# Squares of five norms summed in four bands of 32 output partitions, added one page later

## What is computed

```python
def rmsnorm_2(x, g):
    x32 = x.astype(jnp.float32)
    y = x32 * lax.rsqrt(jnp.mean(x32 * x32, axis=-1, keepdims=True) + EPS)
    return (y * g.astype(jnp.float32)).astype(x.dtype)

def modulate_2(x, g, shift, scale):
    return rmsnorm_2(x, g) * (1 + scale) + shift

def macaron_ffn(xs, g, shift, scale, gate, w_gate, w_up, w_down):
    return xs + 0.5 * gate * swiglu(modulate_2(xs, g, shift, scale), w_gate, w_up, w_down)
```

## Time and profile before

| | us |
|---|---|
| median of 3 runs | 2015.49 |
| lowest and highest | 2014.15, 2018.49 |
| the profiled execution | 2017.46 |
| its span, first to last instruction | 2015.7 |
| TensorE busy | 1955.8 (97%) |
| GpSimd busy | 1304.1 (65%) |
| VectorE busy | 1001.8 (50%) |
| ScalarE busy | 805.8 (40%) |
| mean granted TensorE clock | 0.990 |

### The profile page before, as it was taken

One profiled execution on the slowest core, in us unless ns is written; L12 is line 12 of the kernel. 1 busy time (PEld: TensorE's weight loads), 2 busy tenths in 40 slices (PEclk: granted clock), 3 DMA queues, 4 the chain that ended last, 5 costly groups with the idle time before them and its releaser, 6 DMA issues.

```text
span 2015.7 us, 34549 instructions
## 1 busy us (share of the span) xinstructions
PE 1955.8 (97%) x13934; PEld 1775.3 (88%) x13934; DVE 1001.8 (50%) x2158; ACT 805.8 (40%) x872; POOL 1304.1 (65%) x311
## 2 busy tenths in 40 slices
PE   6999899999999999999999999899999999999998
PEld 4879788877767899999999678799999999999998
DVE  6766455765755554445336435453344334654112
ACT  3443343344445543344333323443344334334332
POOL 5727167766566677777774312387768776867784
PEclk9999899999999999999999899999999999999999
DMA  8537167778987556666664212266666665655442
GB/s 351 220 129 292 61 270 283 303 307 338 364 345 289 222 226 235 245 238 227 240 252 187 105 43 84 105 230 235 239 214 230 239 240 209 251 209 200 178 186 84
DMA packets 63957, 448.74 MB, mean 223 GB/s; under 512 B 7680, under 2 KB 8800, under 8 KB 9824
## 3 DMA queue, kind: packets, MB, share of 16 engines
q1 hardware_dynamic: 61888, 441.65, 58.1%
q10 hardware_dynamic: 1952, 5.44, 0.7%
HBM read 446.01 MB, written 1.05 MB: 222 GB/s over the span
## 4 chain that ended last, share of the span: by engine, by line
PE 53%; issue 23%; POOL 18%; DMA 4%; DVE 1%; ACT 1%; POOLq 0%; SPq 0%; ACTq 0%; DVEq 0%
POOL W L665 15%; PE bank L742 11%; PE bank L744 11%; PE bank L743 11%; DMA raw<-in_pages 3%; PE bank L1194 3%; PE bank L1262 3%; PE bank L1195 3%; PE bank L1202 2%; POOL YC L718 2%; PE bank L768 1%; PE bank L777 1%; PE bank L1137 1%; PE bank L788 1%; PE bank L807 1%
## 5 line engine op out<-in xcount | busy, mean ns | idle before, releaser
L665 POOL TENSOR_TENSOR W<-raw,W 128x2048 fp32r<-128x2048 f32 x220 | 1013.8, 4614 | 516.5 <-ACT W L1561 516.4
L742 PE MATMUL bank<-YH,W 128*128 128x256 f32 x1936 | 551.2, 285 | 1.1 <-POOL W L665 0.8
L744 PE MATMUL bank<-YH,W 128*128 128x256 f32 x1936 | 547.6, 283 | 0.0
L743 PE MATMUL bank<-YL,W 128*128 128x256 f32 x1936 | 547.6, 283 | 0.0
L1561 ACT ACTIVATE W<-raw 128x2048 fp32r<-128x2048 f32 x220 | 420.1, 1909 | 302.0 <-PE bank L744 275.6
L742 PEld LDWEIGHTS bank<-YH,W 128*128 128x128 f32 x1936 | 371.0, 192 | 3.9 <-POOL W L665 1.2
L743 PEld LDWEIGHTS bank<-YL,W 128*128 128x128 f32 x1936 | 371.2, 192 | 0.4 <-issue 0.2
L744 PEld LDWEIGHTS bank<-YH,W 128*128 128x128 f32 x1936 | 371.1, 192 | 0.0
L1916 DVE SCALAR_TENSOR_TENSOR bank<-mraw,CA,bank 128x256 f32<-128x256 f32 x696 | 328.9, 488 | 19.8
L2013 DVE TENSOR_TENSOR bank<-bank,SIL 128x256 f32<-128x256 f32 x110 | 47.6, 432 | 540.2 <-ACT SIL L1580 540.2
L742 PE MATMUL bank<-HH,W 128*128 128x256 f32 x880 | 249.7, 284 | 0.5 <-DVE HL L2015 0.4
(11 more groups left out here) (383 smaller groups left out, 3088.9 us busy)
## 6 DMA issues: line engine op xcount, KB each, us to landing
raw<-in_pages SPq DMA_DIRECT2D x284, 1024.0 KB, 4.8
mraw<-in_mpages SPq DMA_DIRECT2D x98, 1024.0 KB, 6.9
R<-in_pages SPq DMA_DIRECT2D x20, 1024.0 KB, 7.1
XR<-in_pages SPq DMA_DIRECT2D x12, 1024.0 KB, 6.1
R<-in_mpages SPq DMA_DIRECT2D x4, 1024.0 KB, 16.3
HT<-in_acts ACTq DMA_DIRECT2D x1, 1024.0 KB, 14.2
CT<-in_mpages SPq DMA_DIRECT2D x1, 1024.0 KB, 19.3
raw<-in_mpages SPq DMA_DIRECT2D x1, 1024.0 KB, 25.1
```

The source lines that it names most:

```text
L665: nc.gpsimd.tensor_tensor(WL[:, p % SLOTS, :], raw[:, p % SLOTS, :], WH[:, p % SLOTS, :].bitcast(f32), ALU.subtract).then_inc(s_lo, 1)
L742: mm(out, w[0], x[0], start=start, stop=False, skip_group_check=True)
L743: mm(out, w[0], x[1], start=False, stop=False, skip_group_check=True)
L744: return mm(out, w[1], x[0], start=False, stop=stop, skip_group_check=True)
```

## The change

Norms 2 to 6 get their sum in another way. The eight products use 32 columns of ONES and write to four bands of 32 partitions of the bank, tile k to band k % 4, so that each band holds a quarter of the sum. ScalarE copies the bank to XR[:, 0, :], and one product with the whole of ONES adds the bands up. Each quarter then counts 32 times, which the root's scale divides out. That last product stands a page later: for norm 2 a job later, for 3, 4 and 5 after page 0 of the next unit, for 6 at the end of the projection kac0, whose last quarter of products follows the groups. The root of 3, 4 and 5 stands after silu 0 of that unit.

The tiles of norms 3, 4 and 5, and the squares of norm 4, move one unit later on ScalarE and VectorE, and the groups of norm 2 one job earlier. Norm 2's bank is 7 (MISC) in place of 5; in place of the last-but-one scatter it waits for the last modulation sum of the experts. The first four units of ff00 are unrolled, where two were.

```diff
--- before.py
+++ after.py
@@ -329,6 +329,7 @@
                                                   sem("group_aux"), sem("group_aux_copied"))
         s_silu = sem("silu_done")
         s_sq = sem("norm_squares")
+        s_grp, s_grpd = sem("norm_groups_summed"), sem("norm_groups_copied")
         s_rt, s_ri, s_xr, s_yf, s_y = (sem("norm_root"), sem("norm_coef"), sem("norm_scaled"), sem("norm_result"),
                                          sem("norm_split"))
         s_xs = sem("norm_plain")
@@ -416,7 +417,7 @@
         tile("ss1", 1, (MISC,), "act")
         tile("rt", 1, (0,), "dve")
         tile("rtt", 1, (0,), "dve")
-        tile("ss2", 1, (5,), "act")
+        tile("ss2", 1, (MISC,), "act")
         tile("acc_moe", 4, (2, 3, 0, 1), "dve")
         tile("ss3", 1, (MODB,), "act")
         tile("ss4", 1, (MODB,), "act")
@@ -525,6 +526,9 @@
 
         SPLITS = [sum(1 for x in NORMS[:n] if x[1] in OPERANDS) for n in range(len(NORMS) + 1)]
         N_SMALL, N_MID = 10, 4
+        GROUPED = (2, 3, 4, 5, 6)
+        NG4, GW = 4, P // 4
+        TOTAL_IN = {("ctx_ff", 1): 3, ("ctx_ff", 3): 4, ("ff00", 2): 5}
         MID_NORM = {"ctx_ff": ((1, "ss3"), (3, "ss4")), "ff00": ((2, "ss5"),), "ff01": (), "ff10": (), "ff11": ()}
 
 
@@ -535,7 +539,8 @@
                 ("ctx_ff", FF_UNITS, "yc", "acc_ctx", ((1, (ONE, BOTH)), (1, (BOTH, ONE)), (1, (ONE, BOTH)), (1, (BOTH, ONE)),
                                                             (2, (BOTH, BOTH)), (1, (ONE, BOTH)), (1, (ONE, ONE)),
                                                             (1, (BOTH, ONE)), (1, (BOTH, BOTH)), (1, (ONE, BOTH)))),
-                ("ff00", FF_UNITS, "y", "acc_00", ((1, (ONE, ONE)), (1, (ONE, ONE)), (FF_UNITS - 2, (ONE, ONE)))),
+                ("ff00", FF_UNITS, "y", "acc_00", ((1, (ONE, ONE)), (1, (ONE, ONE)), (1, (ONE, ONE)), (1, (ONE, ONE)),
+                                                          (FF_UNITS - 4, (ONE, ONE)))),
                 ("ff01", FF_UNITS, "y", "acc_01", ((2, (ONE, ONE)), (FF_UNITS - 2, (ONE, ONE)))),
                 ("ff10", FF_UNITS, "y", "acc_10", ((2, (ONE, ONE)), (FF_UNITS - 2, (ONE, ONE)))),
                 ("ff11", FF_UNITS, "y", "acc_11", ((2, (ONE, ONE)), (2, (ONE, ONE)), (FF_UNITS - 4, ())))):
@@ -782,6 +787,22 @@
                 for c in range(NCH):
                     norm_chunk(n, c)
 
+            def norm_groups(n):
+
+                ps = opened(pe, f"ss{n}")
+                pe.wait_ge(s_sq, NCH * (n + 1))
+                for k in range(KD):
+                    rows = slice(GW * (k % NG4), GW * (k % NG4 + 1))
+                    last = mm(ps[rows, 0:S], ONES[:, 0:GW], XR[:, k, :], start=(k < NG4), stop=(k >= KD - NG4),
+                              skip_group_check=True)
+                last.then_inc(s_grp, 1)
+
+            def norm_total(n):
+
+                pe.wait_ge(s_grpd, GROUPED.index(n) + 1)
+                mm(bank(f"ss{n}")[:, 0:S], ONES[:], XR[:, 0, :], start=True, stop=True, skip_group_check=True)\
+                    .then_inc(s_tile, 1)
+
             def stay_awake(n):
 
                 for _ in range(8):
@@ -808,7 +829,7 @@
                                   skip_group_check=True)
                 return last
 
-            def linear(p, ps, x, ready=None, k_tiles=KD, wcol=FU, off=0, inc=True):
+            def linear(p, ps, x, ready=None, k_tiles=KD, wcol=FU, off=0, inc=True, behind=None):
 
                 w = shaped([a[:, 0:k_tiles * wcol] for a in arrived(p)], "p (k n) -> p k n", k=k_tiles)
                 for b in range(2):
@@ -816,6 +837,8 @@
                     for k in range(k_tiles):
                         if ready is not None and b == 0:
                             ready(k)
+                        if behind is not None and b == 1 and k == k_tiles // 2:
+                            behind()
                         last = mm3(ps[:, b * S:(b + 1) * S], [a[:, k, c:c + P] for a in w], [a[:, k, :] for a in x],
                                    k == 0, k == k_tiles - 1)
                 if inc:
@@ -850,6 +873,8 @@
                                 last = mm3(PS[GU[j]][:, g * S:(g + 1) * S], [a[:, k, g, :] for a in w],
                                            [a[:, k, :] for a in x], k == 0, k == KD - 1)
                         last.then_inc(s_page, 1)
+                        if j == 0 and (name, u) in TOTAL_IN:
+                            norm_total(TOTAL_IN[name, u])
                     if vectors:
                         for at_unit, ss in MID_NORM[name]:
                             if u >= at_unit:
@@ -1300,23 +1325,26 @@
                         gather(j + 1, e - 5)
                     elif e == 7:
                         aux(j + 1)
+                if t == NJOB - 4:
+                    pe.wait_ge(s_macc, MOD_AT["ctx_ff"])
+                    norm_groups(2)
                 if t == NJOB - 3:
-                    pe.wait_ge(s_scd, 4 * (GSLOTS - 2))
-                    norm(2)
+                    norm_total(2)
             turn_hid(NJOB - 1)
             down(NJOB - 1)
 
 
             def mid_norm(name, u, n):
                 pe.wait_ge(s_modev, MOD_AT[name] + u - 1)
-                norm(n)
+                norm_groups(n)
 
             ff_pass("ctx_ff", 2, (lambda: mid_norm("ctx_ff", 1, 3), lambda: None, lambda: mid_norm("ctx_ff", 3, 4)))
             ff_pass("ff00", 4, (lambda: None, lambda: mid_norm("ff00", 2, 5)))
             mod_product(MOD_AT["mixer"] - 1)
 
-            linear(PA["proj_a"], opened(pe, "kac0"), YC, inc=False, ready=lambda k: y_ready(5, k)).then_inc(s_tile, 1)
-            norm(6)
+            linear(PA["proj_a"], opened(pe, "kac0"), YC, inc=False, ready=lambda k: y_ready(5, k),
+                   behind=lambda: norm_groups(6)).then_inc(s_tile, 1)
+            norm_total(6)
             linear(PA["proj_a"] + 1, opened(pe, "kac1"), YC, inc=False).then_inc(s_tile, 1)
             for q in range(2):
                 linear(PA["proj_a"] + q, opened(pe, "kax", q), Y, ready=(lambda k: y_ready(6, k)) if q == 0 else None)
@@ -1540,7 +1568,12 @@
 
             def norm_root(n):
                 ps = filled(act, f"ss{n}")
-                free(f(RT[:, 0:S], ps[:, 0:S], ACT.Sqrt, bias=EPSC[:, 0:1], scale=1.0 / D), f"ss{n}")
+                copies = GW if n in GROUPED else 1
+                free(f(RT[:, 0:S], ps[:, 0:S], ACT.Sqrt, bias=EPSC[:, 0:1], scale=1.0 / (D * copies)), f"ss{n}")
+
+            def norm_groups_copy(n):
+                act.wait_ge(s_grp, GROUPED.index(n) + 1)
+                f(XR[:, 0, :], bank(f"ss{n}")[:, 0:S], ACT.Copy).then_inc(s_grpd, 1)
 
             def norm_scaled(n, ks=range(KD)):
                 src, dst, _, _, sc, sh, vi = NORMS[n]
@@ -1580,6 +1613,8 @@
                         f(SIL[:, j, :], PS[GU[j]][:, 0:S], ACT.Silu).then_inc(s_silu, 1)
                         if p + j + SLOTS < RPAGES:
                             split(p + j + SLOTS, i)
+                        if j == 0 and (name, u) in TOTAL_IN:
+                            norm_root(TOTAL_IN[name, u])
                     if p + 2 + SLOTS < RPAGES and not (u == n - 1 and name in TAIL):
                         split(p + 2 + SLOTS, i)
 
@@ -1673,7 +1708,7 @@
             after(PA["wout"] + 3)
 
             def state_norm():
-                norm_result(3)
+                norm_scaled(3)
                 norm_squares(4)
 
             def expert_split(u, part):
@@ -1760,6 +1795,8 @@
                     act.wait_ge(sem("in_ctx"), 16)
                     act.wait_ge(s_gdown, 32)
                     norm_squares(2)
+                if t == NJOB - 4:
+                    norm_groups_copy(2)
                 if t == NJOB - 3:
                     norm_root(2)
                 if t == NJOB - 2:
@@ -1772,9 +1809,9 @@
             after(PA["ctx_ff"] - 1)
             out_copy(GSLOTS - 1)
             norm_squares(3, "acc_moe")
-            ff_pass("ctx_ff", (state_norm, lambda: None, lambda: norm_result(4)))
+            ff_pass("ctx_ff", (lambda: norm_groups_copy(3), state_norm, lambda: norm_groups_copy(4), lambda: norm_scaled(4)))
             norm_squares(5, "acc_ctx")
-            ff_pass("ff00", (lambda: None, lambda: norm_result(5)))
+            ff_pass("ff00", (lambda: None, lambda: norm_groups_copy(5), lambda: norm_scaled(5)))
             norm_squares(6, "acc_00")
 
             for dst, src in ((BT0, small["bt"][:, 0:BTN]), (BT1, small["bt"][:, BTN:]), (CSB, small["csb"]),
@@ -1792,8 +1829,10 @@
             def key_half(nm, i, q, c):
                 free(f(KA[:, 2 * q:2 * q + 2, c * S:(c + 1) * S], two(filled(act, nm, i)), ACT.Copy), nm, i)
 
+            norm_groups_copy(6)
+            norm_root(6)
             key_half("kac0", 0, 0, 1)
-            norm_result(6)
+            norm_scaled(6)
             key_half("kac1", 0, 1, 1)
             for q in range(2):
                 key_half("kax", q, q, 0)
@@ -2419,9 +2458,9 @@
             residual("acc_moe", (HT, modcol(ADA + 40)))
 
 
```

(4 more changed lines are left out.)

## The result

The changed kernel takes 2017.68 us (median of 12 executions, 2015.97 to 2026.42), the kernel before, in the same session, 2013.77 (12 executions, 2009.86 to 2022.35). The ratio is 1.0026, with a 95% interval from 1.0014 to 1.0038: slower by some 5 us (3.9 by the two medians) where 5.4 less were forecast.

A forecast was written before the change was run, and what follows sets the result against it. TensorE was taken as the bound from 664 to 1110 us. Norms 2 to 6 gave -1.5, -0.3, +0.1, -1.9 and -1.8, together -5.4 us, from the median 2015.49 to 2010.1; range 2005.5 to 2018.0.

The forecast's parts named there:

- Part 1: Norm sums on TensorE: 3.45 us replaced by 1.1 for groups and 0.45 for the total, saving 1.9 a norm.
- bands apart: Rival at the eight narrow products: bands don't run side by side, loads and products queue; 2021.9 us, chance 0.16.
- pairs only: Rival at the eight narrow products: only pairs overlap, 1.95 us a norm; 2014.4 us, no change, chance 0.12.
- the first rival: Same as bands apart: weight loads stand between the narrow products, which keep 3.45 us; 2021.9 us, chance 0.16.
- The copy and the root: ScalarE's 0.4 us copy is hidden in feed-forward passes; the root between two silus needs 5.4 us of 5.76 and fits.
- Part 2: Norms 3 and 4, tiles one unit later: hidden tile at +20.3, TensorE at +18.3, a 2.0 us wait at each.
- NA_: VectorE's gain column, between modulation sum and reciprocal: taken at its median 1.1 us, minimum 0.16, maximum 3.8.
- Part 3: Norms 2, 5 and 6: norm 5 hides by 0.8 us and gains 1.9; norm 6 gains 1.8, norm 2 1.5.
- +17.1: Norm 5 in ff00: us after silu 1 when the hidden tile is ready, against TensorE's arrival at +17.9.
- Norm 6: Keeps its place; squares end just when the groups want them, so 0.1 us is taken off: gain 1.8.
- Norm 2: Groups a job earlier add no wait; 0.4 us lost to the hidden copy before the down product, gain 1.5.
- The clock: Rival at TensorE's 2.0 us waits: a stall lowers the granted clock, one fall giving 2013.1 us; chance 0.15.

The follow-up runs named there:

- bands: Changed kernel with norm 3's narrow products all in one band and norm 4's in two; only its trace is used: 3.57, 1.85 and 1.00 us at norms 3, 4, 5.
- quarters: Changed kernel with each GpSimd subtraction cut into four pieces from ctx_ff on; ratio to the kernel before 0.9991.
- before_held: Kernel before, with only GpSimd held back until VectorE has made the tiles of norms 3, 4 and 5; ratio to the kernel before 1.0028.
- awake: Changed kernel with 17, 17 and 10 small products of ones on TensorE ahead of the waiting units' modulation products; ratio to the kernel before 1.0001.
- held: Changed kernel, but before's tile places, groups after page 1, total inside the down product, root before the last split, GpSimd waiting for the eight tiles; 2005.30 us, ratio 0.9954.
- early_q: Like held, but GpSimd does not wait for the tiles; its subtraction is cut into four pieces from ctx_ff on instead; ratio to the kernel before 1.0015.
- held_again: The kernel held run once more, unchanged; 2006.12 us, ratio to the kernel before 0.9963.

## Why the prediction was wrong

- **The sums** (Part 1): right. 1.19 for the groups (1.1 taken) and 0.43 for the total (0.45 taken), in place of 3.45, save 1.8 a norm, 1.9 forecast. The rivals "bands apart" and "pairs only" fall with bands. The Trainium skill ("TensorE: Matmul & The Clock Gate", Part 3) gives 2.38 times for three column tiles; four gave 3.57 / 1.00 = 3.6 times here. The same part says that a weight load overlaps products only on another row group. Read so, the first rival and its 3.45 us would have come true; the trace, with 1.00, doesn't bear it out for loads into different column bands.
- **The copy and the root**: right. The copy of the groups takes 0.36 us, nobody waits for it, and the root ends between the two silus with 0.9 us to spare (silu 1 at 698.03 waits for TensorE).
- **The tiles of norms 3 and 4** (Part 2): here the sum failed. The mechanism was right, the size was not: 4.04 and 4.03 in place of 2.0. The term is NA_, 3.75 us in place of 1.1, 2.65 too little. I took the median of its durations, 1.1, as if it were a matter of chance, with 3.8 as the far bound. It is no chance: it is what is left of GpSimd's instruction when VectorE gets there, and the phase of the two is fixed by the order of the work. The changed kernel shows 3.75 both times; quarters shows the same place with 0.43 and a wait of 2.22. I had the spread of a factor of twenty on a row and did not ask what VectorE waited for. The other 0.6 went the other way, by the same cause: the tiles' times were taken from rows of before, where the first tile already stood 0.55 us behind GpSimd (1.82 us for three tiles at 727.88, 1.28 for the same three in before_held). In the changed kernel this part was free. All else in the count was met: the sum's end at +9.0, TensorE at +18.3.
- **Norm 5** (Part 3): wrong, 2.42 us of wait where 0.8 to spare were forecast. NA_ took the 1.09 I had counted, but the first tile lost 3.7 us behind GpSimd, of which 0.55 was in the rows already: 3.7 - 0.55 - 0.8 = 2.4. I had written that it could cost up to 2 with a long NA_, and left it out of the sum. The +17.1 there is also not what its terms add up to, which is 16.75; it came out right because the one-vector sum ends at +5.9 (926.47 to 932.36) and not at +5.5. That is luck.
- **Norm 6**: -1.3 in place of -1.8. The Y products came 2 us earlier and met VectorE's low parts, 0.79 us a tile: three waits where before had one. **Norm 2**: some -1.9 by the distance above, -1.5 forecast. In the traces with four bands the distance is 25.4 to 25.9, in the three with the sum of before 28.5 to 28.9. That nothing hides the groups is not shown.
- **The clock**: put down as a rival in place of the forecast, for one fall. It was put at nothing in the sum, and it came on top, at both long waits: 3.7 us in the first trace, 8.3 in the second (there at norm 5 too), and some 5 by awake. After waits of 2.0 to 2.4 us it fell in some traces too (in quarters at norms 4 and 5, not at 3), so even the forecast's own waits of 2.0 would have cost it at times.
- **Sum.** With the measured terms: norms 3 and 4 +7.4, norm 5 +0.6, norm 6 -1.2 make +6.8; measured between the marks, +6.6. With norm 2 it is +4.7, beside +3.9 by the medians and +5.2 by the ratio. What turned -5.4 into this is the waits behind GpSimd, +4.1 at norms 3 and 4 and +2.4 at norm 5, and the clock, +3.7. The measured 2017.68 lies just inside the range, whose upper end was kept for pairs with a long NA_, or two falls of the clock. The clock did fall twice, but on waits twice as long as forecast, and beside a third at norm 5: the range held it by its width, not by its reasons.

What VectorE waits for is told by all traces alike: instructions with two SBUF inputs (the gain column, the tiles) stand until GpSimd's instruction is over; the modulation sum, with its running sum in PSUM, goes at 0.455 us a step beside GpSimd (700.68 + 5.46 for twelve, across 700.30 + 4.62), and so does the reciprocal. The Trainium skill says so ("SBUF — State Buffer", section "Who interferes with whom"): VectorE and GpSimd share a port pair as an exclusive lock for a whole instruction, and a VectorE instruction with two SBUF inputs contends for it with a GpSimd instruction that reads SBUF, as the subtraction does. The traces agree, with 3.75, 4.21 and 5.01 us.

## What to carry to other kernels

Where a small VectorE instruction has durations between 0.16 and 3.8 us, find whose instruction it ends with before taking a mean; then count it by the phase that the changed order gives. Time taken off the bound engine is worth nothing at a place where it covered another engine's chain: the four-band sum saved 1.8 us a norm on TensorE, and paid only once GpSimd was kept away from the eight tiles (held). When an experiment misses, read its trace before its verdict: early_q's numbers spoke for the wrong theory, and its tiles for the right one.

## What was not expected of the hardware

- Products with 32 output partitions, float32, 256 columns: sixteen instructions in 3.57 us in one band, 1.85 in two, 1.00 in four, to the start of the next product.
- VectorE and GpSimd take turns: eight tiles against four pieces (1.25 us each when alone) go one by one, 7.41 us for what takes 3.26 alone. Four small pieces in place of one large one hardly helped (7.62 with one of 4.9).
- After a wait of 4.0 us TensorE's granted clock was at 0.75 to 0.80 over the next 8 to 9 us, part of them at the lower of its two levels (1.2 of 2.4 GHz), although TensorE stood still for only 0.4 of these 17 us. The price is not fixed: the three waits of 4.0, 4.0 and 2.4 us were followed by a loss of 1.4, 2.2 and 0.1 us in the changed kernel's first trace and of 2.6, 2.9 and 2.8 in its second (distance of the modulation products, less the wait and the unit's own time).
- Open: held's gain of 8 us is 4.6 between ctx_ff and the attention; norm 2 is ahead of that stretch and gives some 1.9. The rest may be the attention's clock, which differs between traces of one kernel (held lost 8.5 us there, held_again 3.4, one less the clock summed over 1132 to 1300 us); this was not separated.
